# Sums of the convolution norm made on GpSimd and VectorE, with one product of ones for each, and moved ahead of a weight panel

## What is computed

```
def layernorm(x, g, b):
    mu = jnp.mean(xf, axis=-1, keepdims=True)
    xc = xf - mu
    y = xc * lax.rsqrt(jnp.mean(xc * xc, axis=-1, keepdims=True) + EPS)
    return y * g + b

def hybrid_mixer(h, w_in, ...):
    glu_in, qkv, gates = jnp.split(h @ w_in, ...)
    u = u_val * jax.nn.sigmoid(u_gate)                     # 512 tokens x 512 channels
    u = causal_depthwise_conv(u, conv_w, conv_b)           # 31 taps
    u = jax.nn.silu(layernorm(u, conv_ln_g, conv_ln_b))
    y_conv = u @ w_conv_out
    y_att = stick_breaking_attention(q, k, v) @ w_att_out
    return (sigmoid(g_conv) * y_conv + sigmoid(g_att) * y_att) @ w_o
```

## Time and profile before

| | us |
|---|---|
| median of 3 runs | 1389.14 |
| lowest and highest run | 1387.64, 1390.62 |
| the profiled execution's own time | 1390.62 |
| its span, from the first to the last instruction | 1388.7 |

### The profile page before, as it was taken

The page is one execution under the profiler, slowest core; times in us unless marked ns, Lnnn a source line. Parts: engine busy times, 40 slices in busy tenths (PEclk is TensorE's granted clock), DMA queues, the critical chain, the costliest instruction groups (busy, mean ns, idle before and its releaser), DMA issues.

```text
span 1388.7 us, 19800 instructions
## 1 busy us (share of the span) xinstructions
PE 1359.2 (98%) x7804; PEld 1181.9 (85%) x7804; DVE 987.9 (71%) x1390; ACT 715.5 (52%) x1170; POOL 168.4 (12%) x144
## 2 busy tenths in 40 slices
PE   9999999999999999999999999999799999999997
PEld 7888888788769999998887788888678999998885
DVE  6899899687687788887337855767677878877332
ACT  4466886553465555572225444556455555565221
POOL 3388343200100000004000011100000000000000
PEclk9999999999999999999999999999999999999999
DMA  9422112455702323235332143510211232323221
GB/s 347 160 91 92 46 46 76 152 187 197 267 16 72 112 93 121 92 109 181 135 106 76 67 132 107 145 46 16 105 48 46 99 114 92 122 107 107 91 91 61
DMA packets 43470, 151.78 MB, mean 109 GB/s; under 512 B 5521, under 2 KB 5777, under 8 KB 43250
## 3 DMA queue, kind: packets, MB, share of 16 engines
q1 hardware_dynamic: 42242, 148.65, 31.6%
q0 software_dynamic: 1136, 1.86, 0.6%
HBM read 143.39 MB, written 2.10 MB: 105 GB/s over the span
## 4 chain that ended last, share of the span: by engine, by line
PE 89%; DVE 7%; ACT 3%; issue 1%; POOL 0%; DVEq 0%; ACTq 0%; POOLq 0%
PE ps L1691 27%; PE ps L1692 27%; PE ps L1693 27%; PE ps L1779 1%; PE ps L1841 1%; DVE t_buf L1059 1%; PE ps L2088 1%; DVE w_lo L1025 1%; PE ps L1733 1%; PE ps L1744 1%; PE ps L1745 1%; PE ps L1749 1%; DVE h_lo L1051 1%; ACT w_hi L547 0%; PE ps L2075 0%
## 5 line engine op out<-in xcount | busy, mean ns | idle before, releaser
L1691 PE MATMUL ps<-h_hi,w_hi 128*128 128x256 f32 (+1 forms) x1120 | 374.3, 334 | 3.0 <-ACT sq L775 1.1
L1693 PE MATMUL ps<-h_hi,w_lo 128*128 128x256 f32 (+1 forms) x1120 | 371.9, 332 | 0.0
L1692 PE MATMUL ps<-h_lo,w_hi 128*128 128x256 f32 (+1 forms) x1120 | 371.8, 332 | 0.0
L1025 DVE TENSOR_TENSOR w_lo<-raw,w_hi 128x1024 fp32r<-128x1024 f32 x141 | 183.9, 1308 | 119.8 <-ACT w_hi L547 119.0
L1691 PEld LDWEIGHTS ps<-h_hi,w_hi 128*128 128x128 f32 x1120 | 213.0, 190 | 26.7 <-issue 3.5
L1693 PEld LDWEIGHTS ps<-h_hi,w_lo 128*128 128x128 f32 x1120 | 213.0, 190 | 20.3
L1692 PEld LDWEIGHTS ps<-h_lo,w_hi 128*128 128x128 f32 x1120 | 213.1, 190 | 19.5 <-issue 0.5
L547 ACT ACTIVATE w_hi<-raw 128x1024 fp32r<-128x1024 f32 x141 | 148.1, 1055 | 150.5 <-PE ps L1693 77.8
L1015 DVE TENSOR_TENSOR w_lo<-quads,w_hi 128x1024 fp32r<-128x1024 f32 (+1 forms) x152 | 165.0, 1087 | 72.6 <-ACT w_hi L547 72.6
L547 ACT ACTIVATE w_hi<-quads 128x1024 fp32r<-128x1024 f32 (+1 forms) x152 | 144.2, 949 | 78.3 <-PE ps L1693 76.7
L1692 PE MATMUL ps<-act_lo,w_hi 128*128 128x512 f32 x352 | 137.1, 389 | 0.0
(11 more groups left out here) (304 smaller groups left out, 2282.4 us busy)
## 6 DMA issues: line engine op xcount, KB each, us to landing
quads<-in_ffn_in SPq DMA_DIRECT2D x76, 512.0 KB, 4.5
raw<-in_ffn_out SPq DMA_DIRECT2D x44, 512.0 KB, 3.8
raw<-in_ada SPq DMA_DIRECT2D x32, 512.0 KB, 4.3
raw<-in_qk SPq DMA_DIRECT2D x25, 512.0 KB, 3.7
ada<-in_ada SPq DMA_DIRECT2D x16, 512.0 KB, 7.5
raw<-in_gates SPq DMA_DIRECT2D x16, 512.0 KB, 3.6
raw<-in_v SPq DMA_DIRECT2D x12, 512.0 KB, 3.9
raw<-in_ffn_in SPq DMA_DIRECT2D x12, 512.0 KB, 4.1
```

What stands on the lines that cost most here:

```text
L1025: nc.vector.tensor_tensor(w_lo[SLOT[p]][:], raw[q % RAW][:], w_hi[SLOT[p]][:].bitcast(f32), ALU.subtract).then_inc(raw_used, 1)
L1691: nc.tensor.matmul(out, w[0], v[0], start=start, stop=False, **kw)
L1692: nc.tensor.matmul(out, w[0], v[1], start=False, stop=False, **kw)
L1693: return nc.tensor.matmul(out, w[1], v[0], start=False, stop=stop, **kw)
```

## The change

1. POOL makes one addition more, behind its last tap: tile 2 + tile 3 into `tap_buf[0]`.
2. DVE makes two additions more behind its last tap, in iteration i = 9: `acc` = tile 0 + tile 1, then `acc` + `tap_buf[0]`. PE makes the mean with one product of ones with `acc` instead of four with the tiles.
3. ACT's four squares go ahead of `prepare("gates", 11)`, the split of panel 13, and ahead of `gate_tile(11)`.
4. DVE's four subtractions go ahead of `feed("gates", 11)`, and right behind them stand four operations more, which add up the squares in `acc`. PE makes the mean of squares with one product instead of four. The buffers `sq` are now released by DVE's additions instead of by PE's products.

```diff
--- before.py
+++ after.py
@@ -275,6 +275,7 @@
         a_exp, a_hi_ready, a_ready, pv_done, o_hi, o_ready = (sem("a_exp"), sem("a_hi_ready"), sem("a_ready"),
                                                               sem("pv_done"), sem("o_hi"), sem("o_ready"))
         tap, cv_mean, cv_sub, cv_sq, cv_sum = sem("tap"), sem("cv_mean"), sem("cv_sub"), sem("cv_sq"), sem("cv_sum")
+        cv_pair, cv_add, cv_var = sem("cv_pair"), sem("cv_add"), sem("cv_var")
         cv_rstd, cv_aff, cv_hi_s, cv_ready = (
             sem("cv_rstd"), sem("cv_aff"), sem("cv_hi_s"), sem("cv_ready"))
         s_done, s_max, s_exp, p_ready, t_done = (sem("s_done"), sem("s_max"), sem("s_exp"), sem("p_ready"),
@@ -476,6 +477,8 @@
                 if n >= 2:
                     pool.wait_ge(pool_tap, n - 1)
                 nc.gpsimd.tensor_tensor(conv[:, c, :], conv[:, c, :], tap_buf[n % 3][:], ALU.add).then_inc(pool_tap, 1)
+            pool.wait_ge(pool_tap, len(SUM_ORDER))
+            nc.gpsimd.tensor_tensor(tap_buf[0][:], conv[:, 2, :], conv[:, 3, :], ALU.add).then_inc(cv_pair, 1)
 
 
             pool.wait_ge(x_again, 16)
@@ -696,20 +699,20 @@
             products(4)
             gate_tile(KT)
             for i in range(KT + 1, 2 * KT):
-                prepare("gates", i)
-                if i == 9:
-                    products(len(SUM_ORDER))
-                gate_tile(i)
                 if i == 11:
                     for c in range(CT):
                         act.wait_ge(cv_sub, c + 1)
                         if c >= 2:
                             act.wait_ge(cv_sum, c - 1)
                         nc.scalar.activation(sq[c % 2][:], conv[:, c, :], ACT.Square).then_inc(cv_sq, 1)
+                prepare("gates", i)
+                if i == 9:
+                    products(len(SUM_ORDER))
+                gate_tile(i)
                 if i == 12:
                     prepare("gates", 13)
                     tables(LN_EXP_TABLES)
-                    act.wait_ge(cv_sum, CT)
+                    act.wait_ge(cv_var, 1)
                     link(nc.scalar.activation(rstd[:], ps[:, CV_VAR, :], ACT.Ln, bias=eps[:], scale=float(D // 512)))
                     nc.scalar.activation(rstd[:], rstd[:], ACT.Exp, scale=-0.5).then_inc(cv_rstd, 1)
                     for c in range(CT):
@@ -1243,15 +1246,27 @@
                 taps(4)
             head_lo(HEADS - 1, qk_hi, qk_lo, o_hi, o_ready)
             for i in range(KT + 1, 2 * KT):
-                feed("gates", i)
-                if i == 9:
-                    taps(len(TAP_ORDER))
                 if i == 11:
                     dve.wait_ge(cv_mean, 1)
                     for c in range(CT):
                         nc.vector.scalar_tensor_tensor(out=conv[:, c, :], in0=ps[:, CV_MEAN, :],
                                                        scalar=-float(D // 512), in1=conv[:, c, :], op0=ALU.mult,
                                                        op1=ALU.add).then_inc(cv_sub, 1)
+                    for c in range(CT):
+                        dve.wait_ge(cv_sq, c + 1)
+                        if c:
+                            dve.wait_ge(cv_sum, c)
+                            nc.vector.tensor_tensor(acc[:], acc[:], sq[c % 2][:], ALU.add).then_inc(cv_sum, 1)
+                        else:
+                            nc.vector.tensor_copy(acc[:], sq[0][:]).then_inc(cv_sum, 1)
+                feed("gates", i)
+                if i == 9:
+                    taps(len(TAP_ORDER))
+                    dve.wait_ge(tap, len(TAP_ORDER))
+                    nc.vector.tensor_tensor(acc[:], conv[:, 0, :], conv[:, 1, :], ALU.add).then_inc(cv_add, 1)
+                    dve.wait_ge(cv_pair, 1)
+                    dve.wait_ge(cv_add, 1)
+                    nc.vector.tensor_tensor(acc[:], acc[:], tap_buf[0][:], ALU.add).then_inc(cv_add, 1)
                 if i == 13:
                     dve.wait_ge(cv_rstd, 1)
                     for c in range(CT):
@@ -1889,17 +1904,11 @@
             for i in range(KT + 1, 2 * KT):
                 gate(i)
                 if i == 11:
-                    pe.wait_ge(tap, len(TAP_ORDER))
-                    pe.wait_ge(pool_tap, len(SUM_ORDER))
-                    for k in range(CT):
-                        ins = nc.tensor.matmul(ps[:, CV_MEAN, :], ones_d[:], conv[:, k, :], start=k == 0,
-                                               stop=k == CT - 1)
-                    ins.then_inc(cv_mean, 1)
+                    pe.wait_ge(cv_add, 2)
+                    nc.tensor.matmul(ps[:, CV_MEAN, :], ones_d[:], acc[:], start=True, stop=True).then_inc(cv_mean, 1)
                 if i == 12:
-                    for k in range(CT):
-                        pe.wait_ge(cv_sq, k + 1)
-                        nc.tensor.matmul(ps[:, CV_VAR, :], ones_d[:], sq[k % 2][:], start=k == 0, stop=k == CT - 1)\
-                            .then_inc(cv_sum, 1)
+                    pe.wait_ge(cv_sum, CT)
+                    nc.tensor.matmul(ps[:, CV_VAR, :], ones_d[:], acc[:], start=True, stop=True).then_inc(cv_var, 1)
 
             pe.wait_ge(o_ready, HEADS)
             for m in range(KT):
```

## The result

| | before | changed |
|---|---|---|
| median, us (9 runs each) | 1390.2 | 1395.58 |
| lowest to highest | 1387.64 to 1393.92 | 1391.69 to 1398.27 |
| ratio, with 95% interval | | 1.0036 (1.0026 to 1.0046) |
| span of the profiled execution | 1388.7 | 1394.3 |

A forecast was written before the change was run, and what follows sets the result against it. PE, never waiting in the stretch, was taken as the bound. Terms -2.57, +3.3, -2.76, +1.4 and +4.2 sum to +3.6 us: 1392.7 us against the median of 1389.14; range 1388.9 to 1396.2, the forecast's own 1391.5 to 1394.

The forecast's parts named there:

- What PE saves: On PE, two passes instead of eight per sum: 2.57 us for the mean, 2.76 for the squares, 5.33 in all.
- The held tap: On DVE, one more convolution tap held beside POOL's extra addition: 1.04 us, bounds 0 and 1.04.
- The mean and gate(12): PE starts the mean at 258.2 instead of 256.31 and gate(12) at 260.5 instead of 259.74; the mean's saving is gone.
- Subtractions and squares: On DVE, subtractions from 260.25, then copy and three additions in 3.1 us, free at 265.75; gate(13) at 268.2 instead of 268.83.
- The loads: SP issues three loads at 267.0, 268.1 and 269.25; panel 15's, the third, lands after 5.0 us at 274.25.
- The triple: Earlier trace's loads issued at 256.60, 257.74 and 258.88, landing after 3.7, 4.3 and 5.0 us; used to price panel 15's load.
- The chain and the merge: Root, multiplication, SiLU and merge panel move by 4.26 us; PE starts the merge at 288.75 instead of 285.18, +3.6 us.
- rival A: The clock falls while PE idles ahead of the merge, adding 1.7 to 2.7 us: about 1394.9; chance 0.27.
- if the clock falls behind it: Sign that the prediction is wrong: the clock falling behind PE's wait of some 4 us ahead of the first merge product.
- B: No tap is held (-1.04) or panel 15 lands after 3.7 (-1.3), or both: 1390.4 to 1391.6; chance 0.22.
- C: PE does not wait for the merge panel's chain; its own arrival at the merge decides: -0.6 us, 1388.5; chance 0.08.
- D: DVE's additions for the mean end by 256.2, so the saved passes stay saved: -5.33 us, 1383.8; chance 0.06.

The follow-up runs named there:

- order_only: Kernel before with only the order changed: subtractions and squares ahead of panel 13 and its ada item, sums still eight passes on TensorE; ratio 1.0038 (1.0025 to 1.0050).
- squares_only: Changed kernel with the mean's part undone: four products of ones again, no GpSimd addition, neither of VectorE's two; ratio 1.0042 (1.0029 to 1.0054) to the kernel before.
- mean_only: Kernel before with the mean's part alone: GpSimd's addition, VectorE's two, one product; squares and order as before; ratio 1.0028 (1.0017 to 1.0039).
- ada_first: Changed kernel with one ada item moved back ahead of the subtractions on VectorE; ratio 1.0037 (1.0024 to 1.0051) to the kernel before.
- root_first: Changed kernel with ScalarE's split of panel 15 moved behind the first SiLU tile, VectorE's items moved to match; ratio 1.0011 (1.0003 to 1.0020) to the kernel before.
- fillers: Changed kernel with 14 small products of ones on TensorE ahead of the first merge product; ratio 1.0024 (1.0015 to 1.0033) to the kernel before.
- sums_only: Changed kernel's sums in the old order, panel 13 and its ada item ahead of subtractions and squares; ratio 1.0036 (1.0023 to 1.0050) to the kernel before.

## Why the prediction was right, and where not

*What PE saves.* 5.33 us of passes: both products are two passes, and no other PE work went. Right, and right that none of it reaches the end.

*The held tap.* One tap more at 1.77 us beside POOL's extra addition; the seven taps take 7.82 instead of 6.80 us, 1.02 more against 1.04. The runs bear the cause out: 6.79 and 6.80 in order_only and squares_only, which lack that addition, 7.83 in mean_only, which has it. VectorE's timeline in the changed kernel answers to the earlier trace rows:

```profile
248.69 7.82 DVE L1138 SCALAR_TENSOR_TENSOR conv<-u_pad,cols,conv 128x512 f32<-128x512 f32 x7
256.55 0.69 DVE L1266 TENSOR_TENSOR acc<-conv 128x512 f32<-128x512 f32 x1
257.35 0.69 DVE L1269 TENSOR_TENSOR acc<-acc,tap_buf 128x512 f32<-128x512 f32 x1
...
265.47 1.22 DVE L1022 SCALAR_TENSOR_TENSOR raw<-raw,c_all 128x1024 f32<-128x1024 f32 x1
```

*The mean and gate(12).* 258.09 and 260.46 against 258.2 and 260.5. Right. The 260.35 given for the end of panel 12's remainder is 0.1 below its own terms (258.1 + 1.14 + 1.22 = 260.46); it ended at 260.32.

*Subtractions and squares.* VectorE past the sums at 265.47 against 265.75: I had priced the copy as an addition (0.78), and it takes 0.42. Gate(13) 267.98 against 268.2.

*The loads.* Out at 266.73, 267.86 and 269.01 against 267.0, 268.1 and 269.25; the third landed after 4.8 against 5.0. The triple was the right row, and ada_first fits it.

*The chain and the merge.* 288.42 against 288.75, so +3.24 against +3.6. root_first shows that 2.03 us of it come from the root standing behind panel 15's load; order_only and squares_only show that the merge is late without the mean's part too.

*The clock.* This is the term that I put at nothing in the sum and kept as rival A, with 0.27 against 0.37. In the profiled execution the clock fell behind the long wait and cost 1.7 us, the low end of A's 1.7 to 2.7. By the prediction's own sign ("if the clock falls behind it") the forecast failed there and A held, though 1395.58 lies in the stated range. Against A I had set that PE works at full rate up to the wait; it did so in the changed kernel, order_only and squares_only, and the clock fell in all three.

The medians alone don't decide between the two. Of the 2.9 us between 1392.7 and 1395.58, 1.1 is the kernel before, which measured 1390.2 over nine runs and not 1389.14. As differences, the forecast is +3.6, A +5.8, and measured is +5.0 (3.6 to 6.4): between them, with both inside the interval or at its edge. What decides is the clock in the traces, one execution of each kernel.

Rivals B, C and D did not come about. That the mean's own saving is gone, mean_only shows for the part alone.

## What to carry to other kernels

Work taken from the bound engine is a gain only while its inputs stay in time: before moving a sum to VectorE, list what stands behind it in that engine's order, down to the loads that its buffer releases trigger, and find the nearest panel with little slack. A buffer released late comes back as a load issued late, and bunched with others it also lands late. Where TensorE can't be spared a wait like the one of 3.87 us here, try a few small products in it: in the trace of fillers, 14 of 128 columns kept the clock at 1.00 and the last sum came 1.7 us earlier.

## What was not expected of the hardware

The fall of the clock is not tied to one place. A wait of 3.87 us brought it in the changed kernel, 3.48 in order_only, 3.59 in squares_only and 4.48 in sums_only; one of 3.33 in ada_first did not. Two waits of 1.57 and 1.25 us with one product between them brought it in root_first, and not in the five other kernels that have them. The window from 790 to 812 us, which the change doesn't touch, has 0.92 in the kernel before, 1.00 in the changed one and 0.84 in ada_first. Single traces of this kernel therefore differ by a microsecond or two outside the stretch, which is why the starts in the stretch and the last sum behind it say more than a span.
